# Attention's value products on pairs of query tiles, with the high and low values side by side in one stationary

## The reference, cut to what matters

```python
def block(qb):                       # layer 0; layer 1 adds the forget terms to sc
    sc = (jnp.einsum('bqhd,bshd->bhqs', qn, k_nope)
          + jnp.einsum('bqhe,bse->bhqs', qr, kr)).astype(jnp.float32) * MLA_SCALE
    sc = jnp.where(kchunk[None, :] <= qchunk[:, None], sc, NEG)
    pr = jax.nn.softmax(sc, axis=-1).astype(v.dtype)
    return jnp.einsum('bhqs,bshd->bqhd', pr, v)
```

## Time and profile before

| | us |
|---|---|
| median of 3 runs (3260.56 to 3261.89) | 3261.38 |
| the profiled execution, its own time | 3267.74 |
| its span, first to last instruction | 3266.0 |
| TensorE busy | 3078.8 (94%) |
| VectorE busy | 1998.0 (61%) |
| ScalarE busy | 979.1 (30%) |
| GpSimd busy | 1450.5 (44%) |

### The profile page before, as it was taken

The page is one execution under the profiler, slowest core; times in us unless marked ns, Lnnn a source line. Parts: engine busy times, 40 slices in busy tenths (PEclk is TensorE's granted clock), DMA queues, the critical chain, the costliest instruction groups (busy, mean ns, idle before and its releaser), DMA issues.

```text
span 3266.0 us, 59087 instructions
## 1 busy us (share of the span) xinstructions
PE 3078.8 (94%) x21250; PEld 2982.2 (91%) x21250; DVE 1998.0 (61%) x3648; ACT 979.1 (30%) x2255; POOL 1450.5 (44%) x943
## 2 busy tenths in 40 slices
PE   7898999998999999998888999999899999999987
PEld 6888999998999999998887988889899999999887
DVE  5555777556556556556564577763665565565664
ACT  3233676533000000003443167653400000000242
POOL 4222454555334334335555445554643343343564
PEclk9999999998999999999998999999899999999988
DMA  3387444220111111112102565531111111111111
GB/s 109 129 301 249 131 119 119 84 84 28 52 45 45 45 45 50 40 39 72 33 27 96 158 165 135 131 88 66 46 45 45 45 45 45 45 51 39 66 33 53
DMA packets 163118, 264.68 MB, mean 81 GB/s; under 512 B 95040, under 2 KB 108880, under 8 KB 162624
## 3 DMA queue, kind: packets, MB, share of 16 engines
q1 hardware_dynamic: 163008, 263.21, 26.4%
HBM read 197.74 MB, written 65.42 MB: 81 GB/s over the span
## 4 chain that ended last, share of the span: by engine, by line
PE 82%; DVE 7%; issue 3%; ACT 2%; POOL 2%; DMA 2%; SPq 1%; ACTq 0%; DVEq 0%; POOLq 0%
PE ps L1261 30%; PE ps L975 15%; PE ps L976 14%; PE ps L977 14%; PE ps L1152 4%; DVE sublayer_out L1975 1%; PE ps L1122 1%; PE ps L996 1%; PE ps L1010 1%; PE ps L1123 1%; DVE act_lo L1990 1%; POOL pre_sums L834 1%; DMA kA_lo<-stage_lo 1%; DVE pre_sums L1951 1%; DVE stage_lo L2071 1%
## 5 line engine op out<-in xcount | busy, mean ns | idle before, releaser
L807 POOL TENSOR_TENSOR weight_hi<-weight_raw,ones 128x1024 fp32r<-128x1024 f32 x185 | 366.5, 1981 | 1187.8 <-PE ps L977 616.3
L2202 DVE TENSOR_TENSOR sublayer_out<-ps,sublayer_out 128x352 f32<-128x352 f32 x1008 | 527.9, 524 | 519.2 <-PE ps L977 510.5
L1261 PE MATMUL ps<-act_hi,weight_hi 128*128 128x352 f32 x2112 | 686.7, 325 | 10.0 <-ACT ffn_act L1656 4.8
L1261 PE MATMUL ps<-act_hi,weight_lo 128*128 128x352 f32 x2112 | 684.7, 324 | 0.0
L1261 PE MATMUL ps<-act_lo,weight_hi 128*128 128x352 f32 x2112 | 684.3, 324 | 0.0
L975 PE MATMUL ps<-act_hi,weight_hi 128*128 128x352 f32 (+2 forms) x1392 | 474.5, 341 | 49.0 <-POOL weight_lo L812 20.5
L812 POOL TENSOR_TENSOR weight_lo<-weight_raw,weight_hi 128x1024 fp32r<-128x1024 f32 x197 | 486.9, 2471 | 38.9 <-ACT weight_hi L1646 24.4
L874 POOL TENSOR_TENSOR probs<-probs,row_inv 128x1024 f32<-128x1024 f32 (+8 forms) x288 | 310.6, 1093 | 354.0 <-DVE row_inv L2149 353.9
L976 PE MATMUL ps<-act_lo,weight_hi 128*128 128x352 f32 (+2 forms) x1392 | 460.2, 331 | 0.0
L977 PE MATMUL ps<-act_hi,weight_lo 128*128 128x352 f32 (+2 forms) x1392 | 459.8, 330 | 0.0
L1261 PEld LDWEIGHTS ps<-act_hi,weight_hi 128*128 128x128 f32 x2112 | 399.9, 189 | 14.0 <-issue 6.9
(11 more groups left out here) (172 smaller groups left out, 6188.6 us busy)
## 6 DMA issues: line engine op xcount, KB each, us to landing
weight_raw<-units SPq DMA_DIRECT2D x201, 512.0 KB, 3.5
k_hi<-kB_hi SPq DMA_DIRECT2D x32, 328.0 KB
qA_hi<-stage_hi SPq DMA_DIRECT2D x16, 528.0 KB, 2.7
qA_lo<-stage_lo SPq DMA_DIRECT2D x16, 528.0 KB, 4.0
q_hi<-qA_hi SPq DMA_DIRECT2D x16, 528.0 KB
q_lo<-qA_lo SPq DMA_DIRECT2D x16, 528.0 KB
kA_hi<-stage_hi SPq DMA_DIRECT2D x8, 656.0 KB, 3.4
kA_lo<-stage_lo SPq DMA_DIRECT2D x8, 656.0 KB, 5.0
```

Source lines behind the costliest of these rows:

```text
L807: pool.tensor_tensor(wh[:, slot, :], wraw[:, slot, :], ones[:, 0:1].to_broadcast((P, UW)), ALU.mult).then_inc(w_hi[slot], 1)
L1261: mm = nc.tensor.matmul(ps[:, 3 * slot + b, 0:TB], a, x, start=(k == 0 and pas == 0), stop=(k == KD - 1 and pas == 2))
L2202: V.tensor_tensor(y[:, m, c], src, y[:, m, c], ALU.add).then_inc(f_acc, 1)
```

## The change

The key blocks of a head's tiles are arranged in five runs, `RUNS = [(6, 7), (0, 1), (4, 5), (8,), (2, 3)]`. In a run of two tiles the blocks alternate between the two tiles for each key block, and the last block is the larger tile's alone. This gives 11 chunks per head, turned at the steps `RUN_STEPS` (counted from the head's first). The stationary operand of a product is now one key block's values, high and low side by side (128 columns, tile `v_both`); it meets the high and then the low probabilities of both tiles (256 columns), or of one tile. The result stands on 128 partitions: the high values' part on the first 64, the low values' part on the last 64. The low output is now made by two VectorE operations, the second waiting for the first (`at_oadd`): the low values' part minus the high output, then the high values' part added. Low values by low probabilities are thereby included. SyncE loads the values as before, the same four transfers, into the new tile.

```diff
+RUNS = [(6, 7), (0, 1), (4, 5), (8,), (2, 3)]
+RUN_STEPS = [5, 5, 6, 6, 7, 8, 9, 10, 11, 12, 12]
+def blocks_of(run):
+    if run == (8,):
+        return [(k, 8) for k in range(3)]
+    a, b = run
+    return [(k, t) for k in range(b) for t in (a, b)] + [(b, b)]
+
 CHUNKS = []
-for _s in range(PAIR):
-    _i = ORDER[_s % STEPS]
-    _n = 3 if _i == 8 else _i + 1
-    CHUNKS += [(_s, _i, _k, min(4, _n - _k)) for _k in range(0, _n, 4)]
-HC = len(CHUNKS) // 2
+for _run in RUNS:
+    _all = blocks_of(_run)
+    CHUNKS += [(_run, _all[_k:_k + 4], _k == 0, _k + 4 >= len(_all)) for _k in range(0, len(_all), 4)]
+HC = len(CHUNKS)
...
+        osum, o = at("out_partial", [P, 512], F32, o)
...
                 def pv(i, c, first):
-                    _, tile, k0, n, last = chunk(c)
+                    run, of, begins, ends = chunk(c)
                     hp = c // HC
-                    if k0 == 0:
-                        need = part_needed(tile, hp)
+                    if begins:
+                        need = part_needed(min(run, key=ORDER.index), hp)
                         if need is not None and not (first and need <= 0):
                             pe.wait_ge(at_olo, i * 6 + (3 * layer * H + need))
...
-                    for j in range(n):
-                        ...
-                        mm = three(out, vh[hp % 2][0:kr, vt, :], vl[hp % 2][0:kr, vt, :], pth[0:kr, turn_slot(c), j, 0:M],
-                                   ptl[0:kr, turn_slot(c), j, 0:M], kt == 0, last and j == n - 1)
+                    def products(kt, j, n, tile, kr, M):
+                        halves = vv[hp % 2][0:kr, kt if tile < 8 else 8 + kt, :, :].rearrange("p x d -> p (x d)")
+                        q0 = tile % 4 * P if tile < 8 else 0
+                        out = ps[:, 6 + tile // 4 if tile < 8 else 7, q0:q0 + (n - 1) * P + M]
+                        for h, buf in enumerate((pth, ptl)):
+                            p = buf[0:kr, turn_slot(c), j:j + n, 0:M]
+                            mm = nc.tensor.matmul(out, halves, p.rearrange("p t q -> p (t q)") if n > 1 else p[:, 0, :],
+                                                  start=kt == 0 and h == 0, stop=ends and j + n == len(of) and h == 1)
+                        return mm
...
-                        for c in chunks_of(s - T_LAG):
+                        for c in chunks_at(s):
...
-                        V.tensor_tensor(dst, src, out_part(c, i, nh)[0].bitcast(F32), ALU.subtract).then_inc(at_olo, 1)
+                        V.tensor_tensor(part, src_lo, out_part(c, i, nh)[0].bitcast(F32), ALU.subtract).then_inc(at_oadd, 1)
+                        dve.wait_ge(at_oadd, i * 6 + (3 * layer * H + n))
+                        V.tensor_tensor(dst, src, part, ALU.add).then_inc(at_olo, 1)
```

More of the change, by code:

```diff
@@ L215, in chunk, with step_of, chunks_at, last_turn @@
 def chunk(c):
[L217 to L225, removed]
+    return CHUNKS[c % HC]
+def step_of(c):
+    return max(ORDER.index(t) for t in chunk(c)[0]) + c // HC * STEPS
+def chunks_at(s):
+    return [h * HC + k for h in (-1, 0, 1) for k, x in enumerate(RUN_STEPS) if h * STEPS + x == s]
+def last_turn(s):
+    tile = ORDER[s % STEPS]
+    return s // STEPS * HC + max(k for k, x in enumerate(CHUNKS) if tile in x[0])
 def turn_slot(c):
@@ L513, in turned @@
         def turned(c, buf):
-            _, i, _, n, _ = chunk(c)
+            run, of, _, _ = chunk(c)
+            n = len(of)
             v = ps[:, 4 + c % 2, :].rearrange("p (t q) -> p t q", q=P)
-            if i < 8:
+            if run != (8,):
                 return [(buf[:, turn_slot(c), 0:n, :], v[:, 0:n, :])]
@@ L520, in turned, with last_tile, out_part @@
                     (buf[0:DEC, turn_slot(c), 2, 0:DEC], v[0:DEC, 2, 0:DEC])]
-        def out_part(c, i, buf):
-            _, tile, _, _, last = chunk(c)
+        def last_tile(c):
+            return max(chunk(c)[0], key=ORDER.index)
+        def out_part(c, i, buf, half=0):
+            tile = last_tile(c)
             hp = c // HC
@@ L537, in is_out @@
         def is_out(c):
-            return chunk(c)[4] and chunk(c)[1] in OUT_AFTER
+            return chunk(c)[3] and last_tile(c) in OUT_AFTER
         block = ctx.enter_context(nc.Block())
@@ L1143, in turn @@
                 def turn(i, c, first):
-                    s, tile, k0, n, _ = chunk(c)
-                    M = P if tile < 8 else DEC
-                    if tile < 8:
+                    run, of, _, _ = chunk(c)
+                    M = P if run != (8,) else DEC
+                    if run != (8,):
                         turn_waits(i, c, first)
-                    for j in range(n):
-                        kt = k0 + j
+                    for j, (kt, tile) in enumerate(of):
                         kr = P if (tile < 8 or kt < 2) else DEC
@@ L1168, in pv @@
                     pe.wait_ge(at_lo, i * (2 * HC) + (base_c + c + 1))
-                    M = P if tile < 8 else DEC
-                    if tile < 8:
-                        out = ps[0:VD, 6 + tile // 4, (tile % 4) * P:(tile % 4 + 1) * P]
-                    else:
[L1173 to L1177, removed]
-                        mm = three(out, vh[hp % 2][0:kr, vt, :], vl[hp % 2][0:kr, vt, :], pth[0:kr, turn_slot(c), j, 0:M],
-                                   ptl[0:kr, turn_slot(c), j, 0:M], kt == 0, last and j == n - 1)
+                    def products(kt, j, n, tile, kr, M):
[7 more added lines that the diff above has]
+                        return mm
+                    if run == (8,):
+                        for j, (kt, tile) in enumerate(of):
+                            mm = products(kt, j, 1, tile, P if kt < 2 else DEC, DEC)
+                    else:
+                        for j in range(0, len(of), 2):
+                            kt, tile = of[j]
+                            mm = products(kt, j, min(2, len(of) - j), tile, P, P)
                     mm.then_inc(at_pv, 1)
@@ L1630, in pair @@
                                 exps(i, todo.pop(), first)
+                        while todo:
+                            exps(i, todo.pop(), first)
                     if drain:
@@ L2160, in outs @@
                         dve.wait_ge(at_ohi, i * 6 + (3 * layer * H + n))
-                        V.tensor_tensor(dst, src, out_part(c, i, nh)[0].bitcast(F32), ALU.subtract).then_inc(at_olo, 1)
+                        hp, src_cols = c // HC, src.shape[-1]
+                        part = osum[64 * (hp % 2):64 * (hp % 2) + VD, 0:src_cols]
+                        _, src_lo, _ = out_part(c, i, nl, 1)
+                        if not (isinstance(i, int) and i == 0 and n == 1):
+                            dve.wait_ge(at_olo, i * 6 + (3 * layer * H + n - 1))
+                        V.tensor_tensor(part, src_lo, out_part(c, i, nh)[0].bitcast(F32), ALU.subtract).then_inc(at_oadd, 1)
+                        dve.wait_ge(at_oadd, i * 6 + (3 * layer * H + n))
+                        V.tensor_tensor(dst, src, part, ALU.add).then_inc(at_olo, 1)
                 def pair(i, first, drain=False):
```

28 lines of the change are left out of this document (15 added, 13 removed).

## The result

The changed kernel takes 3372.6 us (3369.6 to 3376.2 in four runs) against 3261.0 (3260.3 to 3261.9): ratio 1.0343, 95% interval 1.0325 to 1.0361. It is 112 us slower; 3370 was forecast. The profiled execution took 3372.9 us, its span is 3370.9.

What follows compares the result with a forecast made beforehand. TensorE was taken to bound layer 0's attention, with VectorE level in layer 1 after the change. Saved products and two added waits gave 60 us more, 3322 us; the falling clock added 48, making 3370 us, range 3303 to 3412.

Steps and rivals of the forecast that it cites:

- What bounds the kernel, and what is saved: Attention: layer 0 lasts as long as TensorE issues; value products fall from 7.0 to 5.4 us, saving 1.6 a head.
- The first wait: Step 12: TensorE waits 2.35 us a head before the sample's products for the output of tiles 4 to 7.
- The second wait: Before turning chunk 4, ended by chunk 2's low part: 1.5 us a head in layer 0, 2.3 in layer 1.
- The sum at full clock: Heads of 21.8 us in layer 0 and 20.4 in layer 1, 60 us more for both layers together.
- The clock: Falls to 1.2 GHz after the first wait in some five heads of six: 1.5 us a head, 48 us.
- I take 1.7: Us added to a head by 1.2 GHz after the first wait, before multiplying by 5/6.
- Full clock (3322): Rival: the clock stays full after the first wait, 3322 us; chance 0.24.
- Hidden wait (3203): Rival: chunk 7's output is done before TensorE reaches the sample's products, so the kernel is faster, 3203 us; chance 0.06.
- VectorE as the bound everywhere: Rival: VectorE limits both layers, a head takes 18 to 19 us, near no change, 3250 to 3265 us; chance 0.04.
- Clock low for most of a head (3400 to 3430): Rival: the low clock costs 2.3 us or more in each head, the later wait adding to it; chance 0.08.

Runs made afterwards that it cites:

- own_bank_one_op: number 5 with a single VectorE operation per low output, the low values' part left out; 3220.7 us (0.9874 against the kernel before).
- Number 7: Changed kernel's order and pairs of tiles, but three products on 64-column stationaries and one VectorE operation per low output; 3324.6 us (1.0187).
- number 4: Values side by side and two VectorE operations per low output, but the kernel before's order with one tile per product; 3325.9 us (1.0229).
- Number 8: Changed kernel with the last two chunks of a pair of heads in buffers 0 and 1 instead of 2 and 3; 3368.7 us (1.0320).
- number 2: Changed kernel with 16 unused matmuls of 256 columns on constants filling TensorE's wait ahead of the sample's products; 3346.0 us (1.0256).
- number 1: Changed kernel with its last two runs exchanged, so the sample's tile comes after tiles 2 and 3; 3315.8 us (1.0166).
- number 5: number 1 with the sample's products written to score bank 3 instead of bank 7; 3264.8 us (1.0005 against the kernel before).
- number 11: Same run as own_bank_one_op: number 5 with one VectorE operation per low output; 3220.7 us (0.9874).
- spread: number 5 with the head's chunks turned at steps 4, 5, 5, 6, 7 instead of 5, 5, 6, 6, 7; 3244.7 us (0.9948).
- spread_slots: spread with the last two chunks of a pair of heads in buffers 0 and 1 instead of 2 and 3; 3247.6 us (0.9960).

## Why the prediction was right, and where its terms were off

**What bounds the kernel, and what is saved.** Right. TensorE's work was the length of a head; the new paces are the ones read from the scores' forms. In layer 0 own_bank_one_op shows 144.63/8 = 18.1 us of TensorE work a head at the full clock, 18.0 was worked out. The guess was right too that a product of 32 columns goes by the row of 128: 0.11. The Trainium skill (TensorE: Matmul & The Clock Gate, Back-to-back issue gap) gives 0.056 us for an isolated matmul of 128 columns; by that figure the narrow products would have taken half. Number 7 shows 0.06 for 128 columns on a stationary of 64 columns, and number 4 0.11 in a row of them on one of 128; in the changed kernel the first of two is followed after 0.06 and the second after 0.11. So the figure fits one form here and the other only in part.

**The first wait.** Right in place, releaser and chain; 2.35 us was forecast, 2.18 and 2.78 measured, mean 2.48. The excess is a term that was left out: in odd heads the high part of chunk 9 waits for products 7 through their shared buffer. Number 8 takes two thirds of that away, 0.19 us a head on average. In even heads the wait is shorter than forecast because TensorE's own work in the chain takes 1.38 us instead of 1.2. The gap between the chained operations was taken from a stage in which the second starts 0.03 us after the first's end; here it is 0.13 (466.61 + 0.69 to 467.43). The output copy to VectorE is 0.83 (465.78 to 466.61) instead of 0.78. Both are offset by ScalarE, whose high part starts 0.65 after the turning instead of 0.72, and whose copy starts 0.52 after the high part instead of 0.60.

**The second wait.** It is there, ended by the low part as forecast. Layer 0: 1.5 forecast, 1.3 measured. Layer 1: 2.3 forecast, 1.2 measured. The term that went with it was off the other way: layer 1's own work was put at 15.8 us a head after the change (17.4 less 1.6), and own_bank_one_op, at the full clock too but for one part in a hundred, has 133.04/8 = 16.6. The subtraction of a third score pass at 0.23 us for 512 columns took off some 0.8 too much, as the earlier trace rows already showed: TensorE was busy for 145.73/8 = 18.2 us a head in layer 1, not 17.4, and 18.2 - 1.6 is the 16.6 measured.

**The sum at full clock.** Forecast 60 us, some 86 by number 2. The step that was mis-sized: a head at the full clock was to be 21.8 and 20.4 us; number 2 has 22.4 and 21.4. In layer 0 TensorE's own work is 162.23/8 = 20.3, less 1.9 of fillers 18.4 instead of 18.0, and the first wait 2.5 instead of 2.35. In layer 1 the own work is 151.13/8 - 1.9 = 17.0 instead of 15.8, the second wait 1.7 instead of 2.3.

**The clock.** It fell with 29 of 30 waits; five of six were forecast from the stretches in the earlier trace rows and a count. (Of the waits of 2.4 to 3.7 us at 2.4 GHz the trace of the kernel before has eleven, ten of them with 1.2 GHz within 2 us, not nine and eight.) Forecast 48 us, some 27 measured. The step "I take 1.7" was too large: the 3.3 us a head at 1.2 GHz in layer 0 lengthen the head by about 1.0 (23.4 against 22.4). TensorE's busy time is 157.12/8 = 19.6 us against the 18.4 of number 2 without its fillers, 1.3 more, and its idle time 0.25 less; in layer 1 the busy time is 1.3 more as well (18.3 against 17.0), but the waits shrink by 0.7 and the head is only 0.6 longer. So the slower work fills part of the waits, which the prediction allowed for with half of tile 4's scores only. The two errors, 26 short and 21 over, cancelled by luck; the forecast time is closer than its parts.

**The rivals.** Full clock (3322): refuted by the clock's windows, and number 2, made to be that case, has 3346. Hidden wait (3203): refuted by the wait's row. Its condition, two products' groups apart, was met by number 1 and was not enough, since the bank's next owner was then the one that waited. VectorE as the bound everywhere: not in the changed kernel; but once the bank's wait was gone (number 5) the time was 3265, the top of that rival's range, and number 11 shows its second operation priced at a microsecond a head. It works by bursts, not by its sum: spread, with the same operations in other steps, gains 19 us by the ratios. Clock low for most of a head (3400 to 3430): no, it is low for some 3.3 of 23.4 us in layer 0 and 4.8 of 22.0 in layer 1.

**What stays open.** In spread TensorE is busy 147.89/8 = 18.5 us a head in layer 0, where 18.1 was shown with one operation; the records don't show where the 0.4 lies, and modelled ends may hide short waits. Its profiled execution was the longest of its five, but that of spread_slots, at 3240.4, has 147.43/8 = 18.4 too. The clock still falls after some heads of layer 1 (0.97 in its window) with waits of 0.9 us at most, and no run was made for that.

## What to carry to other kernels

When an accumulator's bank is handed from one output to the next, count the work of the matmul engine between the last product into it and the next owner's first, and hold it against the whole chain copy, subtraction, addition; a change that saves work on the engine and shortens that distance at the same time can lose what it saves several times over. Here a swap of the order moved such a wait to the bank's next owner, and a free bank removed it. After it, look for bursts: an engine with 3 us of slack a head can still cost 1 us a head if its work comes in the same steps.

## What was unexpected in the hardware

- A product's pace depended on the width of its stationary: in a row of equal products 128 columns were followed by the next after 0.06 us on a stationary of 64 columns (number 7) and after 0.11 on one of 128 (number 4), and on the latter 32 and 256 columns took 0.11 and 0.12 us. Directly behind a product of 256 columns one of 128 was followed after 0.06 there too (488.32 to 488.38).
- The clock did not fall at a fixed distance from a wait: after the one that ends at 491.78 it was 1.00 for 2.1 us and 0.52 in the 3.3 us after those, and in the odd head before that one it was 0.50 from 0.7 us ahead of the wait's end. Over the 30 waits the fall came from some 1 us before the end to 2.3 us after it.
- The second of two dependent VectorE operations with 512 columns on 64 partitions, which both read TensorE's results, started 0.13 us after the end of the first; the pair in the feed-forward stage 0.03 us.
